# A recurrent, attention and mixture-of-experts layer: the solve in 64x64 blocks, modulation sums in the projection, a new front and tail

## The reference, cut to what matters

```python
mod = silu(c) @ ada_w + ada_b            # 6 rows of 1024: sh1, sc1, g1, sh2, sc2, g2
h   = rms_norm(x, norm1) * (1 + sc1) + sh1
zp  = h @ w_in                           # rwkv 1024 | pool 256 | q, k, v 512 each, f 8
mixed = concat(rwkv7(zp), pool(zp), forgetting_attention(zp))
x   = x + g1 * (mixed @ w_out)
h   = rms_norm(x, norm2) * (1 + sc2) + sh2
x   = x + g2 * moe(h)                    # top 4 of 32 experts, clamped SwiGLU, d_ff 1024
out = rms_norm(x, norm_f)
# rwkv7: 4 heads of 64; state = state*w + (state @ -kk)(kk*a) + v k, read with r
# moe: y[token] += gate * (act(x w_gu + b_gu) w_down + b_down)
```

## Time and profile before

| | |
|---|---|
| median of 3 runs | 1794.33 us (1792.41 to 1797.99) |
| the profiled execution: time | 1798.34 us |
| its span, first to last instruction | 1796.5 us |
| mean granted PE clock | 0.936 of full speed |
| busy: PE, DVE, ACT, POOL | 1624.1, 1379.3, 985.9, 185.0 us |
| moved | 506.73 MB, 282 GB/s over the span |

### The profile page before, as it was taken

The page is one execution under the profiler, slowest core; times in us unless marked ns, Lnnn a source line. Parts: engine busy times, 40 slices in busy tenths (PEclk is TensorE's granted clock), DMA queues, the critical chain, the costliest instruction groups (busy, mean ns, idle before and its releaser), DMA issues.

```text
span 1796.5 us, 20764 instructions
## 1 busy us (share of the span) xinstructions
PE 1624.1 (90%) x7511; PEld 1224.2 (68%) x7511; DVE 1379.3 (77%) x1145; ACT 985.9 (55%) x805; POOL 185.0 (10%) x223
## 2 busy tenths in 40 slices
PE   6999978878977799999999999999999999999940
PEld 1444357667446578888888888888888888888730
DVE  4216277574647888999999999999999999999946
ACT  3113222221214557777777777777777777777721
POOL 1000121120001001001100110010001001100021
PEclk9999988688987899999999999999999999999975
DMA  8153022224604678999999999999999999999924
GB/s 335 47 222 112 6 94 95 71 87 171 253 24 177 244 304 331 389 394 380 379 383 391 388 370 394 387 381 390 391 381 375 394 390 378 378 400 365 373 107 153
DMA packets 91885, 506.73 MB, mean 282 GB/s; under 512 B 10992, under 2 KB 12320, under 8 KB 41536
## 3 DMA queue, kind: packets, MB, share of 16 engines
q1 hardware_dynamic: 76400, 451.75, 64.6%
q0 software_dynamic: 8848, 33.03, 5.1%
q10 hardware_dynamic: 6592, 21.33, 2.9%
HBM read 477.25 MB, written 28.84 MB: 282 GB/s over the span
## 4 chain that ended last, share of the span: by engine, by line
PE 84%; DVE 10%; ACT 2%; DMA 2%; issue 1%; ACTq 0%; POOL 0%; DVEq 0%; POOLq 0%
PE ps L1900 59%; PE ps L1195 7%; DVE Wt L913 3%; PE ps L1834 3%; PE ps L1916 2%; PE ps L1879 2%; PE ps L1201 2%; PE ps L1266 1%; PE ps L1889 1%; PE ps L1093 1%; DVE R L1802 1%; PE ps L1258 1%; PE ps L1170 1%; DMA pool_w<-in_pool_w 1%; PE ps L1244 1%
## 5 line engine op out<-in xcount | busy, mean ns | idle before, releaser
L1420 DVE TENSOR_TENSOR w_lo<-w_raw,w_hi 128x2048 fp32r<-128x2048 f32 x384 | 866.7, 2289 | 93.3 <-ACT w_hi L1414 93.3
L1414 ACT ACTIVATE w_hi<-w_raw 128x2048 fp32r<-128x2048 f32 x384 | 736.4, 1919 | 287.6 <-PE ps L1900 287.6
L1900 PE MATMUL ps<-w_hi,xTh 128*128 128x512 f32 x1024 | 407.3, 398 | 2.7 <-DVE w_lo L1420 2.2
L1900 PE MATMUL ps<-w_lo,xTh 128*128 128x512 f32 x1024 | 401.2, 392 | 0.0
L1900 PE MATMUL ps<-w_hi,xTl 128*128 128x512 f32 x1024 | 275.3, 391 | 0.0
L1900 PEld LDWEIGHTS ps<-w_hi,xTh 128*128 128x128 f32 x1024 | 193.9, 189 | 53.4 <-issue 13.7
L1900 PEld LDWEIGHTS ps<-w_hi,xTl 128*128 128x128 f32 x1024 | 193.1, 189 | 40.9
L1900 PEld LDWEIGHTS ps<-w_lo,xTh 128*128 128x128 f32 x1024 | 193.7, 189 | 38.7
L1900 PE MATMUL ps<-w_hi,aTh 128*128 128x512 f32 x512 | 205.0, 400 | 5.7 <-issue 5.7
L1900 PE MATMUL ps<-w_lo,aTh 128*128 128x512 f32 x512 | 201.8, 394 | 0.0
L1900 PE MATMUL ps<-w_hi,aTl 128*128 128x512 f32 x512 | 159.0, 392 | 0.0
(11 more groups left out here) (362 smaller groups left out, 1553.2 us busy)
## 6 DMA issues: line engine op xcount, KB each, us to landing
w_raw<-in_moe_w_gu SPq DMA_DIRECT2D x256, 1024.0 KB, 6.4
w_raw<-in_moe_w_down SPq DMA_DIRECT2D x128, 1024.0 KB, 7.0
Wt<-in_ada_w SPq DMA_DIRECT2D x24, 1024.0 KB, 5.3
y_rows<-R ACTq DMA_DIRECT2D x32, 512.0 KB, 7.1
Wt<-in_w_in SPq DMA_DIRECT2D x5, 2048.0 KB, 11.1
y_rows<-Wt POOLq DMA_DIRECT2D x1, 7680.0 KB, 25.9
R<-in_x SPq DMA_DIRECT2D x2, 2048.0 KB, 12.8
Wt<-in_w_out SPq DMA_DIRECT2D x1, 4096.0 KB, 15.4
```

What stands on the lines that cost most here:

```text
L1414: nc.scalar.activation(w_hi[:, at[-1] % HI_SLOTS, :], w_raw[:, at[-1] % RAW_SLOTS, :], ACT.Copy).then_inc(hi_rdy, 1)
L1420: nc.vector.tensor_tensor(w_lo[:, s, :], w_raw[:, s, :], w_hi[:, at[-1] % HI_SLOTS, :].bitcast(F32), ALU.subtract).then_inc(lo_rdy, 1)
L1900: ins = mm(ps[:, bank0 + c, :], x[:, k, :], w[:, 512 * (banks * i + c):512 * (banks * i + c) + 512], start=(first and i == 0 and x is xh a ...
```

## The change

- **Front.** x is loaded first. DVE adds all eight chunks, the last in four pieces; 16 matmuls against unit columns (`eye`) put the sixteen 128-blocks on 16 partitions; one copy, one transpose give `modc`. The constants of DVE move behind the scaling of `hT`.
- **Late columns.** They are loaded as 16 pieces of 2048 columns into three buffers, between the `w_in` blocks. `acc` is one DVE operation per piece, one behind each `rw`, `q` and `k` job; the `ada` jobs come four and four, after the first `q` and the first `v`.
- **Solve.** A job holds two tiles as 64x64 blocks, chunk cc on partitions 64cc to 64cc+63; all four tiles go through the levels together. Masks are 64 wide.
- **Experts.** The first chunk of expert 1 is split before its step. `bias_down` is in banks 6 and 7 after the first, after the sixth gate/up chunk.
- **Tail.** Experts 30 and 31 stay on chip (`y_tail`). DVE prepares row numbers, gates and a gate matrix between steps 4 and 5; PE transposes it in step 31 (`tail_turn`) and multiplies it with `y_tail` (`tail_add`). All other rows are gathered before the last product; tile 3 is summed with diagonal matmuls. SP writes the output.

```diff
+        for n in range(8):
+            steps += [("rw", n)] + acc(n)
+        steps += [("q", 0)] + turned(ADA_FIRST)
+        for n in range(4):
+            steps += ([("q", n)] if n else []) + acc(8 + n)
...
-            solve += [(kind, t, par) for kind in ("MP", "M", "NP") for par in range(2)]
-        for lv in range(1, LEVELS):
-            solve += [("T", 2 * q + j, lv) for j in range(2)]
...
+    for lv in range(1, LEVELS):
+        solve += [("T", q, lv) for q in range(2)]
+        if lv <= len(fill):
+            solve += fill[lv - 1]
+        for q in range(2):
+            if lv < LEVELS - 1:
+                solve.append(("XA", q, lv))
+            solve.append(("XB", q, lv))
...
+            def late_load(i):
+                if i == 0:
+                    sp.wait_ge(ada1_mm, 1)
+                if i >= 3:
+                    sp.wait_ge(ada_acc, i - 1)
...
+                sp.dma_start(late[i % 3], ada_v[:, i % KT, n:n + 2 * D]).then_inc(late_in[i % 3], 16)
...
+                if n == 1:
+                    for i in range(5):
+                        late_load(i)
...
+                elif n in (2, 3, 4):
+                    for i in ((5, 6, 7, 8), (9, 10, 11, 12), (13, 14, 15))[n - 2]:
+                        late_load(i)
...
+            for c in range(MT_):
+                if c % 4 == 0:
+                    pe.wait_ge(ada1_sum, c // 4 + 1)
+                ins = mm(ps[0:MT_, 0, 0:P], eye[:, c, :], ada_c[KT - 1][:, P * c:P * c + P], start=(c == 0),
+                         stop=(c == MT_ - 1))
...
+                    for i in range(2 * RH):
+                        for cc in range(2):
+                            r = slice(CHUNK * cc, CHUNK * cc + CHUNK)
+                            t, hc = 2 * q + i // RH, slice(HD * (i % RH), HD * (i % RH) + HD)
+                            lhs, rhs = {"T": (ML[q][r, i, :], X[q][r, i, :]), "XA": (XT[q][r, i, :], Tm[q][r, i, :]),
...
+                            ins = mm(b[r, CHUNK * i:CHUNK * i + CHUNK], lhs, rhs, start=True, stop=True)
...
-            pool.dma_start(y_d[E * BLK:NB * BLK, :].rearrange("(b p) d -> p b d", p=P),
+            pool.dma_start(y_d[(E - 2) * BLK:NB * BLK, :].rearrange("(b p) d -> p b d", p=P),
...
-            def step(n, s, where, nxt, yn, t=None):
+            def step(n, s, where, nxt, yn, t=None, last=False):
...
+                    if t is not None and c == 5:
+                        pe.wait_ge(bd_ev, t)
+                        if yn is not None:
+                            pe.wait_ge(y_ev, yn)
+                        bias_down(t)
...
-                if t is not None:
-                    bias_down(t)
                 if nxt is not None:
-                    if t is not None:
-                        pe.wait_ge(bd_ev, t + 1)
                     xt(n + 1, 1 - s, nxt)
+                if last:
+                    tail_turn()
...
+            def tail_add(t, i, start, stop):
+                for c in range(2):
+                    ins = mm(ps[:, 2 * t + c, :], tailT[:, i, P * t:P * t + P], y_tail[i][:, 512 * c:512 * c + 512],
+                             start=start, stop=stop)
...
+            pe.wait_ge(y_last, 1)
+            tail_add(0, 0, True, False)
+            tail_add(1, 0, True, False)
             pe.wait_ge(at_lo, E)
-            pe.wait_ge(y_ev, E - 1)
+            tail_add(2, 0, True, False)
...
+            for t in range(TT - 1):
+                tail_add(t, 1, False, True).then_inc(fin_mm, 1)
+            t = TT - 1
+            tail_add(t, 0, True, False)
+            tail_add(t, 1, False, False)
+            pe.wait_ge(yg_in[t], 16 * TOPK)
+            for k in range(TOPK):
+                for c in range(2):
+                    ins = mm(ps[:, 2 * t + c, :], diag[:, k, :], yg[t][k][:, 512 * c:512 * c + 512], start=False,
+                             stop=(k == TOPK - 1))
```

More of the change, by code:

```diff
@@ L1089, in head @@
                 return HD * (h % 2), h // 2
-            def ada_part(k, lhs, first=False, last=False):
-                for b in range(4):
-                    ins = mm(ps[0:1, b, :], lhs, ada_c[k][:, 512 * b:512 * b + 512], start=first, stop=last)
-                    if last:
-                        ins.then_inc(ada1_mm, 1)
             def turn_x(t):
@@ L1448, in _ @@
                         load(sp, e, c, extra(j, c))
+            for t in range(TT):
+                sp.wait_ge(res_rdy, t + 1)
+                sp.dma_start(out[0, P * t:P * t + P, :], x2[:, t, :]).then_inc(out_done[t % 2], 16)
         @block.gpsimd
@@ L1753, in _, with step @@
                     x_lo(0)
+            for c in range(EARLY):
+                split_lo(dve, place(1, c))
+            bias_down(0)
             dve.wait_ge(sat_rdy, 1)
-            def step(n, where, before, t=None):
-                if t is not None:
-                    bias_down(t)
+            def step(n, where, before, terms=(), done=0):
                 swiglu(n - 1, before(KT - 1))
@@ L1761, in step @@
                 for c in range(KT):
[L1762 removed]
+                    if c >= done:
+                        split_lo(dve, where(c))
+                    for t, at in terms:
+                        if at == c:
+                            bias_down(t)
                 a_lo(n - 1)
```

765 lines of the change are left out of this document (426 added, 339 removed).

## The result

The changed kernel takes **1653.07 us** (median of 4 runs, 1651.64 to 1655.35) against 1793.37 us for the kernel before beside it: ratio 0.9215, 95% interval 0.9194 to 0.9236. The forecast was 1649, with a range of 1628 to 1678. Measured a second time, later, it took 1652.0 us, ratio 0.9192 (0.9180 to 0.9205), and gave a second profile. The profiled run has a span of 1653.5 us (1796.5 before), and the two traces differ by 143.0 us. It is the slowest of its four executions (1655.35 us); the second profile has a span of 1648.5.

A forecast was written before the change was run, and what follows sets the result against it. PE was taken to bound the steady expert loop, DVE's late adds to lead the solve's waits; -11 + 7 - 95 - 12 - 34 = -145 from the 1794.3 us median gave 1649 us, range 1628 to 1678.

The forecast's parts named there:

- Front, -11: Before the first projection matmul: DVE adds all chunks, matmuls follow piecewise, start at 39 instead of 50.0 us; -11 us.
- Projection, +7: Projection stage: eight `ada` jobs arrive from the solve at 0.88 us each, moved sums cost PE nothing; +7 us.
- PE idle in the projection: Sign that the prediction is wrong: it expected 176 us of projection with PE never idle.
- The rival in which the moved sums hold DVE and PE waits at lora: Projection: zero fill and late-column loads collide, so PE waits at lora; +10 us, 1659 us, chance 0.10.
- Solve, -95: Solve with attention: late adds, loads and `ada` jobs leave, 64-wide blocks save matmul time; 210 to 115 us, -95.
- The 64-wide blocks, 32: Solve: half as many pass jobs give 29 us and W jobs 10, less 7 given back for less-covered attention scaling.
- The rival in which they take turns, +22: Solve: array quadrants do not run together when both row halves write one bank; +22 us, 1671 us, chance 0.12.
- Attention as bound: Rival in the solve: attention steps set the pace, waits for scaling 63 us instead of 22; +41, 1690 us, chance 0.10.
- First experts, -12: First four expert steps: bias products in other banks, read between splits, save 14 us, less 2 for tables; -12 us.
- The tables, "+2": Experts: 5.5 us of index and gate tables on DVE between steps 4 and 5, 2.5 us free per step; +2 us.
- Slower rival: Expert loop: DVE's splits shift, PE waits every step and its clock falls; +274 us, 1923 us, chance 0.02.
- Tail, -34: After the experts: last two experts' rows stay on chip, older rows are gathered during the last product; -34 us.

The follow-up runs named there:

- the kernel with the late columns alone: The kernel before, with only the late modulation columns' loads, sums and `ada` jobs moved from the solve into the projection; 1735.37 us, ratio 0.9664.
- the kernel with the four edits: The changed kernel with second `ada` jobs after the third value job, bias readings one a step, tables inside steps, overflow count read early; 1633.16 us, ratio 0.9078.
- the one with all readings spread: The kernel with the four edits, but one bias product and reading in each of steps 1 to 4, none in step 0; 1633.28 us, ratio 0.9081.

## Why the prediction was right, and where not

The total was right, and the direction of every term; two terms were mis-sized the one way and two the other. Front and tail were read in the profile and not taken apart by a run.

- **Front, -11: right.** -10.7 and -12.0. The last sum ends at 33.3, PE's pieces follow, the copy is at 37.56, and 39 was 39.27. DVE's moved constants made no job wait.
- **Projection, +7: short by 4.** The step that failed is "8 x 0.88 = 7.0 us on a PE that never idles". The jobs cost that (PE is busy 7.2 us more), but there are three banks for four of them in a row, and in the second group the fourth waits 3.9 us for DVE to read the first. I had costed DVE for the sums only. "PE idle in the projection" was one of the prediction's own signs of being wrong, and it came true by these 3.9 us. The sums themselves cost PE nothing, as forecast. The zero fill did collide: it took 40.1 us instead of 25.9, and the five late loads issued beside it took 8.3 to 13.6 us to landing, where six others took 4.7 to 5.0; but no job waited. The rival in which the moved sums hold DVE and PE waits at lora is refuted; a wait for DVE came at another place.
- **Solve, -95: mechanism right, size 12 low.** The late columns were worth 75, not 51 + 5 + 7 = 63. What was missed is the clock: 34 us, beside 30 of PE's idle time and 11 of `ada` records. I had used it for a floor but not in the sum.
- **The 64-wide blocks, 32: right as a sum, in part by luck.** The passes were to give 29 and the matmul jobs of the levels and before them gave 28. W was to give 10 and gave 3.5, since its 14 us in the chain were at the low clock and are 7.4 at the full one. The 7 that I gave back for attention steps less well covered did not show as waits. The reason "the levels run once" is also wrong: two passes take the same time, and what counts is that a job holds two tiles.
- **Quadrants.** 35 ns a record was taken from eight records of the recurrence; 960 records have 29. The rival in which they take turns, +22, was made real with one swapped loop and costs 17.
- **Attention as bound: refuted.** The wait for the scaling fell from 22.2 us to 1.0 instead of rising to 63. Most of it had been DVE's late adds: with the late columns moved, and all else as before, it is

```profile
PE ps L1176 <- DVE R L899: 5.7, 6, 1.8
```

- **First experts, -12: -4.4 and -5.8, the worst term, outside its own bounds of -16 to -6.** Steps 0, 1, 2 and 3 were set at 33, 41, 38 and 35.4 and came at 35.0 to 36.4, 40.3 to 40.8, 39.2 to 40.8 and 35.4 to 37.0. The step that failed is the price of a reading by its own operations; DVE's wait for a product not yet made, and the clock after it, were missing. The tables, "+2", cost 5 to 6: I set 5.5 us against 2.5 us free in a step, but they stood before the operations on which the next step's bias and first chunk wait.
- **Slower rival: rightly small.** The lag heals: from the seventh step on a step takes 35.4 us with PE never idle.
- **Tail, -34: right.** -32.1 in this profile, -33.8 in the second. The difference between them is the pause and the clock behind it. Set against the working, DVE's first full-width operation comes 3.6 us late, and its chain then takes 19.3 us instead of 20.5.

## What to carry to other kernels

Price a wait that leaves by both of its costs: the time that TensorE stands idle, and what its clock gives back when the pauses go. Here the second was 34 us beside 30. Price matmuls taken from a stretch at a low mean clock at the full clock too: W's 14 us were 7.4 there. For work that must go on a nearly full engine, the place counts before the amount: 5 us of small operations cost 5 to 6 at the boundary of two steps and nothing five chunks later. Where array blocks of 64 are issued, let neighbours alternate in row and column half; one loop order made 29 or 47 ns a record of it.

## What the runs showed of the hardware that was not expected

The scaling of the attention, one DVE operation from SBUF to SBUF, differs with whether a POOL operation is running when it starts. In the kernel with the late columns alone its 128x512 form lasts 947 ns on average and its 128x128 form 622, in the kernel before 484 and 283. One such operation, and POOL's mask product, both from the kernel with the late columns alone:

```profile
269.46 1.29 DVE L899 TENSOR_SCALAR R<-R,fmx 128x128 f32<-128x128 f32 x1
```

```profile
269.40 1.27 POOL L621 TENSOR_TENSOR Wt<-Wt,lvl 128x512 f32<-128x512 f32 x1 [3.19 <-PE ps L1264]
```

The DVE operation begins 0.06 us behind POOL's and ends 0.08 us behind it: it takes POOL's time, not its own 0.28. All thirty scalings of this stretch fall into two sorts. Twelve begin while a POOL operation runs; they last 0.91 to 1.48 us and end 0.08 to 0.28 us behind it. The other eighteen keep their 0.28 to 0.49 us, six of them with a POOL operation that began 0.14 us after them. The Trainium skill (SBUF — State Buffer, "SBUF: two separate sides") calls the port pair that the two engines share an exclusive lock, which one holds for a whole instruction; it names certain kinds of DVE operations for this, and no run shows of which kind the scaling is. The trace agrees in the main: whichever begins first sets the time, though a lock held to POOL's very end would have the operation above end 0.28 us behind it and not 0.08. POOL is busy as long in the kernel before (36.8 us against 36.1), but there only two of the thirty scalings are long, so what counts is when the two engines meet. In the changed kernel POOL has half as many mask products (18.1 us busy), and the group of all scalings is 529 ns on average instead of 762. No run here took POOL's products away to price this in time.

The expert loop itself is steady to 0.01 us. From the matmul that begins step 6 to the copy after the down product of expert 30, the changed kernel needs 919.5 us, and so do the kernel with the four edits and the one with all readings spread. All differences between these kernels' profiles lie before it, apart from up to 1.7 us in the tail.
